# Twelve of the sixteen 128-column tiles of layer one's input projection made in pairs by a Strassen product, in one Trainium2 kernel

## What is computed

```python
def even_layer(x, ...):                        # layer 0
    proj = rms_norm(x, norm_g) @ w_in          # 1024 -> 3072 columns in six parts of 512
    ...                                        # causal pooling, short gated convolution, two SiLU gates
    return x + jnp.concatenate([y_a, y_b], -1) @ w_out

def odd_layer(x, cos, sin, ...):               # layer 1
    h = rms_norm(x, norm_g)
    c_q, c_kv, k_rope, z = jnp.split(h @ w_in, ...)   # widths 768, 256, 32, 1024
    q = (rms_norm(c_q, q_lat_g) @ w_uq).reshape(B, S, 16, 96)
    kv = (rms_norm(c_kv, kv_lat_g) @ w_ukv).reshape(B, S, 16, 128)
    ...                                        # per-head norms, rotary part, causal attention
    return x + (o * jax.nn.silu(z)) @ w_out
```

## Time and profile before

| | |
|---|---|
| device time, median of 3 runs | 993.14 us (992.8 to 993.23) |
| profiled execution, span | 989.7 us |
| TensorE (PE) busy | 979.4 us, 99% |
| VectorE (DVE) busy | 692.8 us, 70% |
| ScalarE (ACT) busy | 517.7 us, 52% |
| GpSimd (POOL) busy | 280.7 us, 28% |
| layer 1's input projection in the trace | 340.98 to 532.53 us |
| head projections in the trace | 532.53 to 676 us |

### The profile page before, as it was taken

The page is one execution under the profiler, slowest core; times in us unless marked ns, Lnnn a source line. Parts: engine busy times, 40 slices in busy tenths (PEclk is TensorE's granted clock), DMA queues, the critical chain, the costliest instruction groups (busy, mean ns, idle before and its releaser), DMA issues.

```text
span 989.7 us, 15783 instructions
## 1 busy us (share of the span) xinstructions
PE 979.4 (99%) x5916; PEld 763.0 (77%) x5916; DVE 692.8 (70%) x1242; ACT 517.7 (52%) x971; POOL 280.7 (28%) x355
## 2 busy tenths in 40 slices
PE   9999999999999999999999999999999999999998
PEld 7788444444788888888888999997777888887887
DVE  5798899998844433213443799998999999996311
ACT  7443544335232322231334677867999999997000
POOL 0002342240000001100001468876864335551000
PEclk9999999999999999999999999999999999999999
DMA  8310421111154433121102164567587655540322
GB/s 298 59 53 11 112 80 43 43 43 43 64 170 137 139 128 103 52 65 43 43 22 80 49 202 148 212 178 193 107 214 173 150 129 107 108 107 2 117 85 74
DMA packets 165340, 103.65 MB, mean 105 GB/s; under 512 B 75272, under 2 KB 149520, under 8 KB 165008
## 3 DMA queue, kind: packets, MB, share of 16 engines
q1 hardware_dynamic: 159216, 102.25, 36.8%
q10 hardware_dynamic: 6048, 0.39, 0.5%
HBM read 56.48 MB, written 29.36 MB: 87 GB/s over the span
## 4 chain that ended last, share of the span: by engine, by line
PE 78%; DVE 14%; POOL 3%; ACT 3%; issue 2%; DVEq 0%; POOLq 0%; ACTq 0%
PE banks L106 22%; PE banks L108 22%; PE banks L107 22%; PE banks L2086 6%; PE banks L2104 3%; PE banks L2105 1%; DVE heads_y L1886 1%; POOL heads_prod L1992 1%; DVE heads_x L1881 1%; DVE heads_x L1882 1%; DVE heads_probs_big L1895 1%; ACT front_set_b L595 1%; DVE heads_ss L1928 1%; PE banks L2113 1%; ACT heads_probs_big L1768 1%
## 5 line engine op out<-in xcount | busy, mean ns | idle before, releaser
L106 PE MATMUL banks<-front_act_hi,front_w_hi 128*128 128x512 f32 x352 | 139.1, 395 | 0.3 <-DVE front_w_lo L760 0.3
L108 PE MATMUL banks<-front_act_hi,front_w_lo 128*128 128x512 f32 x352 | 137.8, 391 | 0.0
L107 PE MATMUL banks<-front_act_lo,front_w_hi 128*128 128x512 f32 x352 | 137.6, 391 | 0.0
L1903 DVE TENSOR_TENSOR heads_pt_lo<-banks,heads_pt_hi 128x512 f16<-128x512 f32 (+2 forms) x192 | 102.1, 555 | 11.3 <-ACT heads_pt_hi L1777 7.0
L1777 ACT ACTIVATE heads_pt_hi<-banks 128x512 f16<-128x512 f32 (+2 forms) x192 | 88.4, 485 | 4.9 <-PE banks L2086 4.6
L106 PEld LDWEIGHTS banks<-front_act_hi,front_w_hi 128*128 128x128 f32 x352 | 66.5, 189 | 14.9 <-DVE front_w_lo L760 0.5
L107 PEld LDWEIGHTS banks<-front_act_lo,front_w_hi 128*128 128x128 f32 x352 | 66.5, 189 | 14.1 <-issue 0.5
L108 PEld LDWEIGHTS banks<-front_act_hi,front_w_lo 128*128 128x128 f32 x352 | 66.4, 189 | 14.0
L2104 PE MATMUL banks<-heads_v,heads_pt_hi 128*128 128x128 f16 x576 | 74.6, 220 | 0.0
L528 POOL TENSOR_TENSOR front_sq<-front_sq,front_squares 128x1024 f32<-128x1024 f32 x6 | 14.4, 2395 | 199.4 <-ACT front_squares L722 199.4
L2086 PE MATMUL banks<-ident,heads_probs_big 128*128 128x128 f32 x416 | 69.0, 279 | 1.4 <-ACT heads_probs_big L1768 1.3
(11 more groups left out here) (362 smaller groups left out, 2655.1 us busy)
## 6 DMA issues: line engine op xcount, KB each, us to landing
qk_scratch<-heads_y SPq DMA_DIRECT2D x22, 512.0 KB, 3.6
front_w<-in_w_in_c SPq DMA_DIRECT2D x17, 512.0 KB, 4.0
front_x<-in_x_t SPq DMA_DIRECT2D x16, 512.0 KB, 5.5
front_raw<-in_w_in_ab SPq DMA_DIRECT2D x14, 512.0 KB, 5.1
qk_scratch<-heads_last_y SPq DMA_DIRECT2D x10, 512.0 KB, 3.5
front_w<-in_w_out_ab SPq DMA_DIRECT2D x8, 512.0 KB, 3.7
x_scratch<-front_x SPq DMA_DIRECT2D x8, 512.0 KB, 3.9
v_scratch<-heads_v SPq DMA_DIRECT2D x32, 128.0 KB, 2.9
```

What stands on the lines that cost most here:

```text
L106: nc.tensor.matmul(out, w_hi, a_hi, start=first, stop=False, skip_group_check=resumed)
L107: nc.tensor.matmul(out, w_hi, a_lo, start=False, stop=False, skip_group_check=resumed)
L108: return nc.tensor.matmul(out, w_lo, a_hi, start=False, stop=last, skip_group_check=resumed)
L1903: nc.vector.tensor_tensor(pt_lo[:, q % PIECES, :width], t_ps[:, banks[("piece", n, k)] % 3, :width], pt_hi[:, q % PIECES, :width], ALU.sub ...
```

## The change

Layer 1's input projection is done in another order and form. First come gate tiles 0 to 3 and the key tile, plain. Then six pairs: four of the eight latent tiles, two of gate tiles 4 to 7. The six right-hand forms of four chunks are made from layer 1's inputs anew (`right_sums` on GpSimd, `rights` on ScalarE and VectorE), with a peak of the inputs (`x_peak`, `later_top`, `later_scaling`) that TensorE spreads in the first gate tile. The token sums move into the first gate tile, the spread of the roots into the middle of the second. ScalarE writes one more scaled copy of each input chunk (`xg`). The latents are kept without their gain, which `latent_high` and `lat_low` now multiply in. The key tile is turned in the first pair, and the latents' square sums are taken in the fifth. Gates 4 and 5 are scaled by GpSimd once their pair is done, 6 and 7 by VectorE after the last pair, and ScalarE applies SiLU to these four after the pairs. The arrays `latent` and `gate` and the work areas have other places in memory, the pairs' semaphores are passed to the later phase, and a scratch size is set for the DMAs.

```diff
+PLAIN_GATES = 4
+LATER_PAIRS = (KQ + KKV + NK - PLAIN_GATES) // 2
+ALL_PAIRS = 2 * GROUPS + LATER_PAIRS
+FORMS = 7
+SPARE = 14 * 1024
...
+    def all_products(self, eng):
+        eng.wait_ge(self.pair_ready, FORMS * ALL_PAIRS)
+    def banks_left(self, eng, pairs):
+        eng.wait_ge(self.c_done, 3 * pairs)
+        eng.wait_ge(self.c21_done, pairs)
...
+    Z0 = OUT0 + OUT_TILES
+    ROPE0 = Z0 + PLAIN_GATES
+    TILES = ROPE0 + 1
+    GATE_PAIRS = PAIRED + LAT // 2
...
+    EARLY_SPLIT = (1, 2, 3, 4, 0, KQ, KQ + 1, KQ - 1)
...
+            elif p == PAIRED:
+                sp.wait_ge(act_low, RIGHT0 + SIX)
+            elif p == PAIRED + 1:
+                sp.wait_ge(proj_ready, ROPE0)
+            elif p == PAIRED + 2:
+                sp.wait_ge(act_low, RIGHT0 + SIX * CHUNKS)
+                sp.wait_ge(silued, OUT0 + PLAIN_GATES)
...
+        load_pair(PAIRED + 1)
+        load_pair(PAIRED + 2)
+        sp.wait_ge(form_low, FORMS * (PAIRED + 1))
+        sp.wait_ge(row_peak, PAIRED + 1)
+        sp.wait_ge(spread, 2)
         for k in range(KKV):
             sp.dma_start(wide[:, k, :], w_ukv[k * P:(k + 1) * P, :]).then_inc(tail_wide_in, 16)
-        for n in range(LAT0 + RING + 1, LAT0 + 7):
-            load(n)
-        sp.wait_ge(wide_read, 1)
+        for p in range(PAIRED + 3, ALL_PAIRS):
+            load_pair(p)
+        sp.wait_ge(form_low, FORMS * ALL_PAIRS)
...
+            if p == PAIRED:
+                pool.wait_ge(act_low, RIGHT0 + 2 * SIX)
+            elif p:
                 pool.wait_ge(form_low, FORMS * p)
             else:
                 pool.wait_ge(act_low, FIRST_FORMS)
+            if p == PAIRED + 1:
+                pool.wait_ge(silued, OUT0 + 1)
...
+            if c >= 2:
+                pool.wait_ge(act_low, RIGHT0 + SIX * (c - 1))
...
+        for c in range(CHUNKS):
+            right_sums(c)
+        for p in range(PAIRED, ALL_PAIRS):
+            if p == GATE_PAIRS + 1:
+                square_sums(GATE_PAIRS - 1)
+            left_sums(p)
+            if PAIRED + 1 < p <= GATE_PAIRS:
+                square_sums(p - 2)
+        for m in range(2):
+            dest_m = pair_dest(GATE_PAIRS, m)
+            pool.wait_ge(c_done, 3 * (GATE_PAIRS + 1))
+            pool.wait_ge(c21_done, GATE_PAIRS + 1)
+            nc.gpsimd.tensor_tensor(dest_m, dest_m, rstd_all[:], ALU.mult).then_inc(gate_scaled, 1)
...
+            elif p == PAIRED:
+                act.wait_ge(act_low, RIGHT0 + SIX * CHUNKS)
...
+            if p == GATE_PAIRS:
+                act.wait_ge(turned_in, 1)
+            if p == GATE_PAIRS + 1:
+                act.wait_ge(small_ready, 1)
...
+        def rights(c):
+            act.wait_ge(later_scaled, 1)
+            for part in range(SIX):
+                if part >= 2:
+                    act.wait_ge(t_added, STAGED0 + 4 * c + part - 1)
+                nc.scalar.activation(right_split(c, part, 0), right_source(c, part), ACT.Copy,
+                                     scale=later_scale[:, 0:1]).then_inc(act_high, 1)
+        def plain_silu(i):
+            act.wait_ge(evacuated, Z0 + i + 1)
+            nc.scalar.activation(gate[:, i, :], held[i][:], ACT.Silu).then_inc(silued, 1)
...
+        def latent_high(m):
+            if m in (KQ - 1, KQ, KQ + 1):
+                act.wait_ge(roped, 1)
+            elif m == 0:
+                act.wait_ge(form_low, FORMS * ALL_PAIRS)
+            else:
+                act.wait_ge(wide_read, 1)
+            nc.scalar.activation(lat_hi[:, m, :], latent[:, m, :], ACT.Copy, scale=gam_lat[:, m:m + 1]).then_inc(lat_high, 1)
...
+                last_pair = p + 1 == ALL_PAIRS
+                if PAIRED < p <= GATE_PAIRS:
+                    latent_squares(p - 1)
+                snapshot(p, 0)
+                if p == PAIRED:
+                    plain_silu(1)
+                if p == PAIRED + 1:
+                    act.wait_ge(reduced, 2)
+                    nc.scalar.activation(trig[:], red[:], ACT.Sin).then_inc(trig_done, 1)
+                if p == GATE_PAIRS - 1:
+                    latent_high(1)
+                if p == GATE_PAIRS:
+                    latent_high(3)
+                if last_pair:
+                    latent_high(0)
+                snapshot(p, 1)
+                if p == PAIRED:
+                    plain_silu(2)
+                if p == GATE_PAIRS - 1:
+                    latent_high(2)
+                if p == GATE_PAIRS:
+                    latent_high(4)
+                if last_pair:
+                    for m in (KQ, KQ + 1, KQ - 1):
+                        latent_high(m)
+                snapshot(p, 2)
+                if p == PAIRED:
+                    plain_silu(3)
+                if not last_pair:
+                    pair_forms(p + 1, range(FORMS))
+                else:
+                    first_weights()
+                last_quarter(p)
...
+                nc.scalar.activation(xg[m][:], x1[m % RING][:], ACT.Copy,
+                                     scale=gam1[:, m:m + 1]).then_inc(xg_ready, 1)
...
+        rights(0)
+        high(Z0 + 2)
+        rights(1)
+        spread_out(2)
+        high(Z0 + 3)
+        rights(2)
+        rights(3)
+        high(ROPE0)
+        pair_forms(PAIRED, range(FORMS))
+        act.wait_ge(proj_ready, TILES)
+        nc.scalar.activation(krt[0:2 * ROPE, :], proj[0:2 * ROPE, ring_bank(ROPE0)], ACT.Copy).then_inc(lat_out, 1)
+        plain_silu(0)
+        later_paired()
...
+            if p == GATE_PAIRS:
+                dve.wait_ge(lat_summed, LAT - 2)
+                if order:
+                    dve.wait_ge(turned_in, 1)
+            if p == GATE_PAIRS + 1:
+                dve.wait_ge(small_ready, 1)
...
+        def rights(c):
+            for part in range(SIX):
+                dve.wait_ge(act_high, RIGHT0 + SIX * c + part + 1)
+                nc.vector.scalar_tensor_tensor(right_split(c, part, 1), right_source(c, part), later_scale[:, 0:1],
+                                               right_split(c, part, 0), ALU.mult, ALU.subtract).then_inc(act_low, 1)
...
+            for p in range(PAIRED, ALL_PAIRS):
+                last_pair = p + 1 == ALL_PAIRS
+                if not last_pair:
+                    pair_peak(p + 1)
+                if p == PAIRED:
+                    angles(0)
+                if p == PAIRED + 1:
+                    tables()
+                if p == PAIRED + 2:
+                    peaks()
+                if p == GATE_PAIRS - 1:
+                    top()
+                if p == GATE_PAIRS:
+                    v_scales()
+                if not last_pair:
+                    pair_scale(p + 1)
+                else:
+                    rope_and_roots()
+                    for j in range(4, LAT):
+                        lat_low(j)
+                if p == GATE_PAIRS:
+                    lat_low(0)
+                    lat_low(1)
+                if not last_pair:
+                    pair_low(p + 1, [0])
+                quarter(p, 0)
+                if not last_pair:
+                    pair_low(p + 1, [1])
+                quarter(p, 1)
+                if last_pair:
+                    for k in range(KKV):
+                        first_weights(k, "kv", k)
+                    for k in range(KQ - 2):
+                        first_weights(KKV + k, "uq", k)
+                else:
+                    pair_low(p + 1, [2, 3])
+                quarter(p, 2)
+                if not last_pair:
+                    pair_low(p + 1, [4, 5, 6])
+                if p == PAIRED:
+                    angles(1)
+                if p == GATE_PAIRS:
+                    lat_low(2)
+                    lat_low(3)
+            for k in range(KQ - 2, KQ):
+                first_weights(KKV + k, "uq", k)
+            for m in range(2):
+                late_gate(m)
...
+                nc.vector.tensor_reduce(x_peak[:, m:m + 1], xg[m][:], AX_X, ALU.max,
+                                        apply_absolute_value=True).then_inc(x_topped, 1)
+                if m == OUT_TILES - 1:
+                    later_top()
...
+        low(Z0 + 1)
+        later_scaling()
+        rights(0)
+        roots(2, ms1, rstd1, tmp1, sums[:, 0])
+        low(Z0 + 2)
+        rights(1)
+        plain_gate(0)
+        low(Z0 + 3)
+        rights(2)
+        plain_gate(1)
+        low(ROPE0)
+        rights(3)
+        pair_peak(PAIRED)
+        plain_gate(2)
+        pair_scale(PAIRED)
+        pair_low(PAIRED, range(FORMS))
+        plain_gate(3)
+        link(nc.vector.tensor_scalar(eps1[:], ms1[:], EPS, None, ALU.mult))
+        later_paired()
...
+                    if k == CHUNKS:
+                        pe.wait_ge(x_topped, NK + 1)
+                        pe.wait_ge(mixed, GROUPS)
+                        nc.tensor.matmul(pooled[:, BANK:BANK + 1], ones[:], x_row[:], start=True, stop=True).then_inc(x_spread, 1)
+                    if k == NK - 2:
+                        pe.wait_ge(x1_added, OUT_TILES - 1)
```

(29 more changed lines are left out.)

426 lines of the change are left out of this document (236 added, 190 removed).

## The result

The changed kernel takes 1009.54 us (median of 4 runs, 1009.25 to 1009.74) against 992.97 us (median of 4): 1.0173 times as long, 95% interval 1.0159 to 1.0187; the two medians alone give 1.0167. It was forecast 5.5 us faster and came out 16.6 us slower, beyond the range. The profiled execution spans 1007.5 us, 17.8 more than before.

The account below looks back on a forecast made before the run. TensorE was taken as the bound, busy 979.4 of 989.7 us. The terms -20.8 + 6.6 + 1.7 + 2.2 + 0.3 + 4.5 = -5.5 turned a median of 993.14 into 987.6 us, range 977.5 to 992.5.

Parts of the forecast that it names:

- TensorE's own account: Layer one's input projection on TensorE: products removed -130.6, fp16 pair products +108.8, row sums and peak spread +1.0: -20.8 us.
- spread of the roots: Second gate tile: TensorE waits for VectorE's root chain, slowed by GpSimd's sums: +6.6 us, bounds 0 to 8.5.
- clock after it: After the idle of 6.6 us in the second gate tile the granted clock falls: +1.7 us, bounds 0 and 2.
- start of the first pair: Before the first pair: TensorE waits for VectorE to scale gate tile four: +2.2 us, bounds 1.5 and 3.5.
- middle pairs: Pairs between first and last: a 0.2 us quarter wait seen in layer zero, everything else fits: +0.3 us, bounds 0 and 3.
- last pair: Last pair: third snapshot 3.5 us late behind rotary key and roots, head projections start late: +4.5 us, bounds 1 and 7.
- new places of the narrow work: The narrow sums stay, now without key transposes behind them: from -1.7 to 0, taken as 0.
- lock price: Root chain: a small VectorE operation waits for GpSimd's whole sum, making chain and diagonal 7.5 us.
- sign of being wrong: Stated as wrong if the diagonal's wait is under 2 us, middle pairs exceed 19.5, or the head stretch exceeds 145.
- rival without it: Plain tiles' 0.2267 follows into pairs or remaining tiles; only product count pays, 15.5 for 21.8: 993.9 us, chance 0.02.
- slower rival: VectorE bounds the pairs, second quarter late; each of four pairs loses 2 to 2.4 us: 995.6 to 997.6, chance 0.09.
- small-wait rival: Small VectorE operations slip between GpSimd's sums, so waits are small, no clock fall: 976.5 to 979.5 us, chance 0.25.

Follow-up runs that it names:

- experiment 1: Changed kernel with ScalarE's second latent square moved behind the next snapshot in pairs three and four: 997.30 us against 1009.54.
- experiment 2: Changed kernel with GpSimd's latent square sum put ahead of the next pair's four left sums: 999.95 us against 1009.54.
- experiment 3: Changed kernel with the second half of the angles behind the peak, the sine behind pair two's third snapshot, tables in pair four: 1001.26 us.
- experiment 4: Changed kernel with angles left in place, GpSimd's left sums of pair three held until that pair's weight peak is taken: 1005.81 us.
- experiment 5: Changed kernel with GpSimd's four sums of chunk 2 held until the roots stand on their diagonal: 1004.99 us.
- experiment 10: Changed kernel with second square behind snapshot, angles behind peak, tables in pair four, roots, gate scaling and peak earlier, GpSimd's gate products behind last snapshot: 974.52 us.
- experiment 11: As experiment 10, but GpSimd's two gate products held until rotary key and roots are done, not until the third snapshot: 974.71 us.
- experiment 6: Changed kernel with 28 further products, their result overwritten, ahead of the spread of the roots where TensorE was idle: 1005.98 us.

## Why the prediction was wrong, point by point

Against the 191.55 us of before, with what was measured in the changed kernel:

| step of the prediction | forecast | measured |
|---|---|---|
| TensorE's own account (removed, added, row sums) | -20.8 | -20.8 by its distances: 0.2267 and 0.2158 again |
| spread of the roots | +6.6 | +6.4 |
| clock after it | +1.7 | +3.0 |
| start of the first pair | +2.2 | +2.0 |
| **middle pairs** | **+0.3** | **+20.9** (waits 5.6, 4.4, 4.4; clock 6.4) |
| last pair | +4.5 | +4.4 (waits 2.5 and 0.4, clock 1.5) |
| new places of the narrow work | 0 | +1.2, what remains |
| sum | -5.5 | +17.1 |

The clock terms are what the products behind a wait were over the full clock's distance, summed (in pair two 2.8, and 0.3 on the row sum). The last line but one is the remainder, not a measurement of its own.

*The step that failed is "Middle pairs: +0.3. [...] peaks, tops and scales fit."* It checked each engine's total per pair (VectorE 9.4, ScalarE 7.0, GpSimd 5.2 of 18.3 us) and took the one wait that layer zero shows. (The rows that it names for VectorE give 8.9 to 9.3; the difference decides nothing.) It did not walk the queues with the work that is new in layer one. Two things were missed. The second square on ScalarE waits for a GpSimd sum queued behind four others: all three engines have idle time, yet the chain last quarter, square, left sums, square sum, square, snapshot takes 9.5 us where the snapshot is due 5.2 us into the pair. And the angles stand ahead of the peak at the one moment when GpSimd is released. The lock price that was set on the roots was never set on the angles. Experiments 1 and 2 (12.2 and 9.6 us) show the first, 3 and 4 the second. The prediction's own sign of being wrong, middle pairs over 19.5 us, came true in pairs two to four. (Pair five could not take the 18.3 to 18.7 us that it names in any case: the change puts the narrow square sums there, 3.6 us with 1.5 of clock behind them. They are not new, so the sum is not touched.)

*The bounds "0 and 3"* were those of a mean over layer zero's pairs; a step that no row shows in this surrounding should have carried the price of its longest chain.

*The lock and the spread of the roots* were right in mechanism and size: 6.44 us for 6.6, and experiment 5 gives 3.4 us for the chain without GpSimd (2.2 plus 1.23). One of the operations held up there, that of line 92, has one input; the prediction took all of the chain for two-input ones.

*The clock* was mis-sized: 3.0 us and not 1.7 behind the longest wait, beyond its bounds of 0 and 2, and it was counted once where it fell five times on account of waits, behind those of 2.46, 4.42, 4.44, 5.64 and 6.44 us.

*The last pair* came out near its size, 4.4 for 4.5, in part by luck. The place was right: rotary key and roots beside GpSimd's gate products, then the snapshot. But the wait for the snapshot was put at 3.5 and was 2.46, the late weights at 1.0 and were 0.43, and a fall of the clock, 1.5, stood only in the upper bound. *The difference between types* held: 0.2158 us for fp16 and 0.2267 for fp32r stand in the changed kernel too, so the rival without it is out. The formula of the Trainium skill (TensorE: Matmul & The Clock Gate, "Back-to-back issue gap") gives 0.216 for both. The Trainium skill calls it there the gap of a single matmul and puts a sustained stream at about 0.131 us; the streams of this case run at 0.216 and 0.227, so the fp16 rows fit the formula, and for fp32r the measurement decides against both figures.

*The slower rival* named the wrong mechanism: no pair of the changed kernel waits for the second quarter. That wait appeared in experiment 4 (3.0 us) and, in pair four, in experiments 10 and 11 (1.0 us), each time because the scale came late. *The small-wait rival* describes what the change can give once its order is right: 974.5 measured, forecast 976.5 to 979.5 there (its own sum, 993.1 - 20.8 + 4 to 7, is 976.3 to 979.3).

What stays open: why a wait is followed by slow products in one run and not in another. Of the waits before the first pair, 1.96 us was followed by them in experiments 2, 3 and 6 and not in the changed kernel; 3.03 us in experiment 4 was not, 2.19 us in experiment 3 was.

## What to carry to other kernels

When a stretch gets shorter, walk each engine's queue through one period in order, with what each wait is itself queued behind on the other engine; totals per period say little of a chain that crosses three queues. Place narrow chains on VectorE where GpSimd is not let go, and put what TensorE asks for (a peak, a snapshot) ahead of work that nobody awaits. Count half clock on top of a long wait of TensorE: each of the five from 2.46 to 6.44 us in the changed kernel brought 1.5 to 3.1 us more. The same change was 1.7% slower in one order and 1.8% faster in another.

## What the runs showed of the hardware

- Seven narrow VectorE operations took 8.2 us beside GpSimd's sums and 2.0 us alone; in the other direction a GpSimd sum of 1.3 us took 5.58 beside a row of VectorE's low halves.
- The clock's fall can be bought off: 28 useless products in a wait of 6.4 us took away a fall of 3.0 us, and the median is 3.6 us lower.
